# A two-part sequence model on one core: merges of the first block re-ordered and fed early, late convolution taps on GpSimd

## The reference, cut to what matters

```python
y_a = rms_norm(o_gla, norm_w)  * silu(g)      # 4 heads of 64
y_b = rms_norm(o_diff, norm_w) * (1 - lambda_init) * silu(g)   # 4 heads of 128
y_c = rms_norm(o_hgrn, norm_w) * silu(g)      # 4 heads of 64
y = jnp.concatenate([y_a, y_b, y_c], axis=-1) @ w_out[layer]
x = x + rms_norm(y, norm_post[layer])
```

## Time and profile before

| | us |
|---|---|
| median of 3 runs | 4371.12 (4370.69 to 4390.93) |
| the profiled execution | 4380.19 |
| its span, first to last instruction | 4378.4 |
| PE busy | 3314.5 (76%) |
| VectorE (DVE) busy | 2278.0 (52%) |
| ACT busy | 1315.6 (30%) |
| GpSimd (POOL) busy | 492.2 (11%) |

### The profile page before, as it was taken

The page is one execution under the profiler, slowest core; times in us unless marked ns, Lnnn a source line. Parts: engine busy times, 40 slices in busy tenths (PEclk is TensorE's granted clock), DMA queues, the critical chain, the costliest instruction groups (busy, mean ns, idle before and its releaser), DMA issues. The chain is left out here.

```text
span 4378.4 us, 82454 instructions
## 1 busy us (share of the span) xinstructions
PE 3314.5 (76%) x35948; PEld 2727.3 (62%) x35948; DVE 2278.0 (52%) x3684; ACT 1315.6 (30%) x2374; POOL 492.2 (11%) x399
## 2 busy tenths in 40 slices
PE   6998555565769995544749699898776778888499
PEld 6998443244349994442534599797765657777344
DVE  4212984475662216866747512167477845455343
ACT  2111651143331114632433211133244412222341
POOL 0000541110100003421001000000000012222100
PEclk9999656799889995666989899899877869899799
DMA  4232002441332321113123322265422031120331
GB/s 157 87 98 73 21 27 103 152 102 51 114 136 86 99 74 36 31 54 103 39 82 111 132 83 82 104 195 162 160 97 70 33 96 42 42 52 23 146 115 39
DMA packets 260456, 383.97 MB, mean 88 GB/s; under 512 B 46527, under 2 KB 193271, under 8 KB 258684
## 3 DMA queue, kind: packets, MB, share of 16 engines
q1 hardware_dynamic: 155962, 257.35, 18.8%
q10 hardware_dynamic: 104134, 121.36, 8.1%
HBM read 261.66 MB, written 123.13 MB: 88 GB/s over the span
## 5 line engine op out<-in xcount | busy, mean ns | idle before, releaser
L361 PE MATMUL psum<-proj_w_low,h_high 128*128 128x344 f32 (+1 forms) x1984 | 656.5, 331 | 0.0
L361 PE MATMUL psum<-proj_w_high,h_high 128*128 128x344 f32 (+1 forms) x1984 | 654.3, 330 | 0.0
L361 PE MATMUL psum<-proj_w_high,h_low 128*128 128x344 f32 (+1 forms) x1984 | 654.3, 330 | 0.0
L392 DVE COPY proj_y<-psum 128x344 f32<-128x344 f32 (+1 forms) x130 | 70.8, 544 | 782.0 <-PE psum L361 782.0
L361 PEld LDWEIGHTS psum<-proj_w_high,h_high 128*128 128x128 f32 x1984 | 374.8, 189 | 6.6
L361 PEld LDWEIGHTS psum<-proj_w_low,h_high 128*128 128x128 f32 x1984 | 374.6, 189 | 6.0
L361 PEld LDWEIGHTS psum<-proj_w_high,h_low 128*128 128x128 f32 x1984 | 374.3, 189 | 4.5
L417 ACT ACTIVATE proj_y<-psum 128x344 f32<-128x344 f32 (+1 forms) x130 | 61.9, 476 | 694.2 <-PE psum L361 694.2
L800 POOL TENSOR_TENSOR scan_d<-scan_b 128x384 f32<-128x384 f32 x112 | 124.4, 1111 | 1122.4 <-DVE scan_b L646 1115.5
L1312 PE MATMUL psum<-merge_wo,merge_yt 128*128 128x512 f32 x512 | 227.7, 603 | 13.5 <-ACT merge_yt L1257 10.0
L361 PE MATMUL psum<-proj_rest_w_low,h_high 128*128 128x304 f32 x640 | 201.7, 315 | 39.9 <-DVE proj_rest_w_low L381 20.5
(11 more groups left out here) (412 smaller groups left out, 7084.3 us busy)
## 6 DMA issues: line engine op xcount, KB each, us to landing
proj_raw<-in_w_in SPq DMA_DIRECT2D x24, 1376.0 KB, 6.9
proj<-proj_y ACTq DMA_DIRECT2D x192, 172.0 KB, 1.9
delta_x<-dn_qkv SPq DMA_DIRECT2D x40, 384.0 KB, 5.1
proj<-proj_y ACTq DMA_DIRECT2D x68, 224.0 KB, 1.9
dn_prep_x<-proj SPq DMA_DIRECT2D x54, 256.0 KB, 3.6
proj_raw<-in_w_in SPq DMA_DIRECT2D x7, 1792.0 KB, 8.8
norm_x<-x_stream SPq DMA_DIRECT2D x24, 512.0 KB, 3.3
modulate_w<-in_mod_w SPq DMA_DIRECT2D x6, 2048.0 KB, 8.3
```

The lines of the kernel that those rows point to most:

```text
L361: last = PE.matmul(self.ps[:, j % 4, 0:self.width], hp[:, kt, tokens], wp[:, c % 2, kt, :], start=kt == 0 and n == 0, stop=kt == KT - 1 an ...
L392: V.tensor_copy(self.y[:, j % 4, :], self.ps[:, j % 4, 0:self.width]).then_inc(*self.copied[1].inc())
```

## The change

In the first block the weight `w_out` and the constants of a merge get fixed places in SBUF. They are fetched by a stage `Fetch` of six DMAs on SP, woven into the attention ahead of the merge with start 1; `Fetch` waits for them at 10 (so at 11). `Merge1` has no DMA for weight or constants of its own. Its tiles are re-ordered: gates are made two tiles ahead, gates 1 and 2 in one piece after tile 0's copy; the transposes of tile n+1 go ahead of the products of tile n (for tile 1, behind the products of tile 0); `fetch(n + 2)` goes ahead of the load of x.

```diff
-        self.wo, self.hw, self.pw, self.dsc = t("wo", [P, KT, D]), t("hw", [P, D]), t("pw", [P, D]), t("dsc", [P, 1])
+        self.wo, (self.hw, self.pw, self.dsc) = wo, consts
...
-        self.weight, self.consts = sig("dma", "weight", 1), sig("dma", "consts", 14)
...
-        SP, a, L = self.nc.sync, self.a, slice(self.layer, self.layer + 1)
-        for name, w, h0, h1 in (("gla_norm", 64, 0, 4), ("diff_norm", P, 2, 6), ("hgrn_norm", 64, 12, 16)):
-            for h in range(h0, h1):
-                SP.dma_start(self.hw[:, h * w:(h + 1) * w], bc(a[name][L, :], [P, w])).then_inc(*self.consts.inc())
-        SP.dma_start(self.pw[:], bc(a["norm_post"][L, :], [P, D])).then_inc(*self.consts.inc())
-        with self.nc.allow_non_contiguous_dma(reason="one value per partition"):
-            SP.dma_start(self.dsc[:], bc(a["c_layers"][L, 2:3], [P, 1])).then_inc(*self.consts.inc())
+        SP = self.nc.sync
...
         for n in range(NT):
+            if n + 2 < NT:
+                fetch(n + 2)
             if n >= 2:
                 SP.wait_ge(*self.added(n - 2))
             SP.dma_start(self.x[:, n % 2], self.xs[n * P:(n + 1) * P, :]).then_inc(*self.x_loaded[n % 2].inc())
-            if n + 2 < NT:
-                fetch(n + 2)
             yield
...
-        V.wait_ge(*self.consts(13))
         c(V.tensor_scalar(self.hw[:, 256:768], self.hw[:, 256:768], self.dsc[:], None, ALU.mult))
-        for _ in self.dve_gate(0):
-            pass
-        for n in range(NT):
-            V.wait_ge(*self.turned(n))
-            if n >= 2:
-                V.wait_ge(*self.projected(n - 2))
-            V.tensor_copy(self.yt[:, n % 2, 512:1024], self.ps[:, 4 * (n % 2) + 1]).then_inc(*self.copied_v.inc())
-            yield from weave(self.dve_gate(n + 1) if n + 1 < NT else iter(()), self.dve_finish(n - 1) if n else iter(()))
-        yield from self.dve_finish(NT - 1)
-
...
+        self.dve_sums(0)
+        self.dve_gate(0)
+        self.dve_copy(0)
+        for n in (1, 2):
+            self.dve_sums(n)
+            self.dve_gate(n)
+        for n in range(NT + 1):
+            yield n
+            m, s = n - 1, (n - 1) % 2
+            if n + 1 < NT:
+                self.dve_copy(n + 1)
+            if n:
+                V.wait_ge(*self.y_squared(m))
+                V.tensor_scalar(self.ys[:, s:s + 1], self.ys[:, s:s + 1], 1.0 / D, EPS, ALU.mult, ALU.add).then_inc(*self.y_meant.inc())
+            if n and n + 2 < NT:
+                self.dve_sums(n + 2)
+            if n:
+                V.wait_ge(*self.y_rstd(m))
+                V.wait_ge(*self.x_loaded[s](m // 2))
+                V.scalar_tensor_tensor(out=self.y[:, s], in0=self.y_ps(m), scalar=self.ys[:, s:s + 1], in1=self.pw[:], op0=ALU.mult, op1=ALU.mult).then_inc(*self.y_scaled.inc())
+                V.wait_ge(*self.y_scaled(m))
+                V.tensor_tensor(self.y[:, s], self.y[:, s], self.x[:, s], ALU.add).then_inc(*self.added.inc())
+            if n and n + 2 < NT:
+                self.dve_gate(n + 2)
+
+    def dve_copy(self, n):
+        V = self.nc.vector
+        V.wait_ge(*self.turned(n))
+        if n >= 2:
+            V.wait_ge(*self.projected(n - 2))
+        V.tensor_copy(self.yt[:, n % 2, 512:1024], self.ps[:, 4 * (n % 2) + 1]).then_inc(*self.copied_v.inc())
+
...
     def act(self):
         S = self.nc.scalar
-        S.dma_start(self.wo[:], self.a["w_out"][self.layer].rearrange("(k p) n -> p k n", p=P)).then_inc(*self.weight.inc())
-        for _ in self.act_gate(0):
-            pass
-        for n in range(NT):
-            s = n % 2
-            S.wait_ge(*self.turned(n))
-            if n >= 2:
-                S.wait_ge(*self.projected(n - 2))
-            S.activation(self.yt[:, s, 0:512], self.ps[:, 4 * s], ACT.Copy).then_inc(*self.copied_s.inc())
-            yield from weave(self.act_gate(n + 1) if n + 1 < NT else iter(()), self.act_finish(n - 1) if n else iter(()))
...
+        self.act_logs(0)
+        self.act_sigmoid(0)
+        self.act_copy(0)
+        for n in (1, 2):
+            self.act_logs(n)
+            self.act_sigmoid(n)
+        for n in range(NT + 1):
+            yield n
+            m, s = n - 1, (n - 1) % 2
+            ys = self.ys[:, s:s + 1]
+            if n:
+                S.wait_ge(*self.projected(m))
+                if m >= 2:
+                    S.wait_ge(*self.stored[s](m // 2 - 1))
+                S.activation(self.y[:, s], self.y_ps(m), ACT.Square, accum_out=ys).then_inc(*self.y_squared.inc())
+            if n + 1 < NT:
+                self.act_copy(n + 1)
+            if n:
+                S.wait_ge(*self.y_meant(m))
+                self.k.so.chain(S.activation(ys, ys, ACT.Ln))
+                S.activation(ys, ys, ACT.Exp, scale=-0.5).then_inc(*self.y_rstd.inc())
+            if n and n + 2 < NT:
+                self.act_logs(n + 2)
+            if n:
+                S.wait_ge(*self.added(m))
+                S.dma_start(self.xs[m * P:(m + 1) * P, :], self.y[:, s]).then_inc(*self.stored[s].inc())
+            if n and n + 2 < NT:
+                self.act_sigmoid(n + 2)
...
-        PE.wait_ge(*self.weight(0))
-        for n in range(NT):
+
+        def turn(n):
             s = n % 2
...
+        turn(0)
+        for n in range(NT):
+            yield n
+            s = n % 2
+            if n and n + 1 < NT:
+                turn(n + 1)
             PE.wait_ge(*self.copied_s(n))
             PE.wait_ge(*self.copied_v(n))
             if n >= 2:
@@ -1311,9 +1333,8 @@
                 for j in range(8):
                     last = PE.matmul(ps[:, 4 * s + 2 + half], self.yt[:, s, j * P:(j + 1) * P], self.wo[:, j, half * 512:(half + 1) * 512], start=j == 0, stop=j == 7)
             last.then_inc(*self.projected.inc())
-            yield
-
-
+            if n == 0:
+                turn(1)
```

```diff
-        yield 1.6
+        yield self.CONVOLVED
         S.wait_ge(*self.conv(u))
...
+class DeltaPrepareLate(DeltaPrepare):
+
+
+    CONVOLVED = 2.6
+
+    def __init__(self, *args):
+        super().__init__(*args)
+        n = len(self.units)
+        self.tap0, self.tap2, self.tap_added = self.event("pool", "tap0", n), self.event("pool", "tap2", n), self.event("dve", "tap_added", n)
+
+    def pool(self):
+        self.nc.gpsimd.wait_ge(*self.consts(0))
+        yield from self.each(self.pool_unit)
+
+    def pool_unit(self, u):
+        G, s = self.nc.gpsimd, u % 2
+        yield 0
+        G.wait_ge(*self.loaded[s](self.loads[u]))
+        if u >= 2:
+            G.wait_ge(*self.done(u - 2))
+        G.tensor_tensor(self.tmp[:, s], *self.tap(u, 0), ALU.mult).then_inc(*self.tap0.inc())
+        yield 1.3
+        G.wait_ge(*self.tap_added(u))
+        G.tensor_tensor(self.tmp[:, s], *self.tap(u, 2), ALU.mult).then_inc(*self.tap2.inc())
+
+    def convolve(self, u, y, tmp):
+        V = self.nc.vector
+        self.k.vo.chain(V.tensor_tensor(y, *self.tap(u, 1), ALU.mult))
+        yield 1
+        V.wait_ge(*self.tap0(u))
+        V.tensor_tensor(y, y, tmp, ALU.add).then_inc(*self.tap_added.inc())
+        yield 2
+        V.wait_ge(*self.tap_added(u))
+        V.wait_ge(*self.tap2(u))
+        V.tensor_tensor(y, y, tmp, ALU.add).then_inc(*self.conv.inc())
...
-            together(k, (attention, 0, 1.0), *beside)
-            run(k, Merge1(k, layer, p1, o_scan, o_diff, xs))
...
+            fetch = Fetch(k, f"merge1_{layer}", [(wo[:], args["w_out"][layer].rearrange("(k p) n -> p k n", p=P)), *heads,
+                                                 (pw[:], bc(args["norm_post"][one, :], [P, D])), (dsc[:], bc(args["c_layers"][one, 2:3], [P, 1]))])
+            together(k, (attention, 0, 1.0), *beside, (fetch, 1, 1.0))
+            run(k, Merge1(k, layer, p1, o_scan, o_diff, xs, wo, (hw, pw, dsc)))
...
-        together(k, (attention, 0, 1.0), (DeltaPrepare(k, "dn_prep_late", range(6, NT2), p2, dn, attention.top), 2, 1.1))
+        together(k, (attention, 0, 1.0), (DeltaPrepareLate(k, "dn_prep_late", range(6, NT2), p2, dn, attention.top), 2, 1.1))
```

More of the change, by code:

```diff
@@ L1208, in dve_gate, with heads, dve_sums @@
+    def dve_copy(self, n):
[4 more added lines that the diff above has]
+        V.tensor_copy(self.yt[:, n % 2, 512:1024], self.ps[:, 4 * (n % 2) + 1]).then_inc(*self.copied_v.inc())
+    @staticmethod
+    def heads(x, a, b, w):
+        return x[:, a:b].rearrange("p (h d) -> p h d", d=w)
+    def dve_sums(self, n):
+        V, c, s, ss = self.nc.vector, self.k.vo.chain, n % 2, self.ss
         V.wait_ge(*self.o_squared(n))
@@ L1209, in dve_gate @@
         for a, b, w, h in self.HEADS:
-            last = V.reduce_sum(ss[:, s, h:h + (b - a) // w], heads(self.sq, a, b, w), axis=AX)
+            last = V.reduce_sum(ss[:, s, h:h + (b - a) // w], self.heads(self.sq, a, b, w), axis=AX)
         last.then_inc(*self.summed.inc())
@@ L1869, in dve_unit @@
             V.wait_ge(*self.stored[s](self.stores[u - 2]))
[L1870 to L1875 removed]
+        yield from self.convolve(u, y, tmp)
         yield 3.5
```

(12 more changed lines are left out.)

66 lines of the change are left out of this document (23 added, 43 removed).

## The result

The changed kernel took 4312.9 us (median of 4 runs, 4302.5 to 4323.4) against 4374.4 for the kernel before beside it: a ratio of 0.984, 95% interval 0.982 to 0.987. The forecast was 4322. A later comparison on another chip gave 0.986 (0.984 to 0.989). The profiled execution took 4316.56 us, 63.6 less than that of before; the medians lie 61.5 apart. 49.0 were forecast.

The account below looks back on a forecast made before the run. No engine was full overall; late fetches delayed merge starts, TensorE bounded their steady part, and VectorE's convolution work mostly lengthened neighbourhood attention. 47.4 + 0.8 - 1.5 + 2.3 = 49.0 us off 4371.12 gave 4322.1; 8-in-10 range 4302 to 4340.

Parts of the forecast that it names:

- The start of the merges: Both merges: with constants and weight fetched earlier, first gates start 26.1 and 21.3 us sooner, 47.4 us gained.
- The order of the tiles: Merges: 0.83 us a tile gained but used up by two TensorE waits at the start; 0.8 us left in all.
- Beside the attentions: Attentions ahead of the merges: first head delayed 0.5 us, VectorE held longer by the bias addition 1 us; 1.5 us lost.
- The late taps: Neighbourhood attention: two products per unit moved from VectorE to GpSimd gain 12.3 us, less 3, 1 and 6: +2.3 us.
- the prediction's own sign: Listed mark of a wrong forecast: the neighbourhood attention stage at 3163 to 3522 being 10 us shorter or longer.
- the contention: Neighbourhood attention: GpSimd's 24 tap products hold VectorE for an eighth of their 25 us, 3 us lost (0 to 25).
- The wait behind the third pair's addition: Neighbourhood attention: fourth unit's tap 2 queues behind a table addition on GpSimd, holding VectorE 8.8 us; 6 us counted (3 to 9).
- GpSimd's taps pay: Neighbourhood attention: third pair's wait absorbed and taps never meet VectorE, part worth +13 us, time 4311; chance 0.18.
- Taps cost: Neighbourhood attention: taps meet VectorE half the time and the wait costs 9 us, part -10 us, time 4334; chance 0.18.
- VectorE bounds the merge: Merges: VectorE's round is 16 us instead of 14.3, losing 7 to 8 us a merge, time 4337; chance 0.07.
- fetch not hidden: Attentions' first heads delayed 4 us each, addition held badly, merge's first inputs needing 10 us: time 4341; chance 0.05.
- slower than before: Neighbourhood attention: 24 waits for GpSimd hold VectorE over 2.1 us each; at 3 us each, time 4396; chance 0.02.

Follow-up runs that it names:

- e1: Kernel before plus only the early fetch of weight and constants beside the attentions, old tile order and taps: ratio 0.988 to the kernel before.
- e12: Late convolutions' taps 0 and 2 computed by no engine, VectorE making tap 1's product and two additions: 4317.4 us, ratio 0.986 to the kernel before.
- e2: Changed kernel with the late taps back on VectorE, both merge parts kept: ratio 0.987 to the kernel before.
- e4: Changed kernel with GpSimd's tap 2 at 1.1 instead of 1.3, ahead of the third pair's table addition: ratio 0.981 to the kernel before.
- e6: Changed kernel with tap 2 at 1.1 and GpSimd's bias addition cut into 8 pieces: ratio 0.981 to the kernel before.
- e10: Repeat of the changed kernel with tap 2 at 1.1 and the bias addition in 8 pieces: 4295.8 us, ratio 0.981 to the kernel before.
- e3: Kernel before with only the late taps moved to GpSimd: ratio 0.995 to the kernel before.
- e9: The changed kernel run again, unaltered: 4312.3 us, ratio 0.986 to the kernel before.
- e11: Repeat of the changed kernel with the late taps back on VectorE: 4323.0 us, ratio 0.988 to the kernel before.
- e7: Changed kernel with tap 2 at 1.1, later pairs' five transfers 1.5 steps apart and table additions behind them: ratio 0.983 to the kernel before.

## Why the forecast was right, point by point

**The start of the merges** was the right place and the right size: 6.6 us to the first gate were forecast, 7.0 and 6.2 came; transposes at 18.4, 18.7 and 17.9 came. e1 shows that the fetch is 49 of the 50 us that the two merges lost.

**The order of the tiles.** With T = 1098.24, the start of the first transposes, gate 2 ends at T + 23.4 as worked out, TensorE waits 3.92 us (4.0), tile 2's products start at T + 40.9 (41.2), the round is 14.61 (14.8) and the last products end at T + 127.0 (127.9). The second wait, 1.8 us, is hidden in the first merge by tile 1's products, which took 14.9 instead of 13.8 us (the granted clock was 0.63 in their first 2.7 us, and 1.00 from 1126 on); in the second merge there are 2.53 and 2.85 us of waiting and the end is T + 128.0. So 0.4 us a merge was small by a microsecond (1.4 measured), and the reason given for so little holds: most of the steady gain of a microsecond a tile is spent on waits at the start. There VectorE's gates 2 and 3 are the limit. In the steady part VectorE as the bound of the merge is excluded: gates 4 to 6 end 0.8 us ahead of their transposes in both merges, where half a microsecond was forecast.

**Beside the attentions.** -1.5 was forecast, and 1.7 us were lost in the first pair. In the mean of all profiles the first attention is 2.5 us longer with the fetch than without (249.9 us in eight against 247.4 in three; the addition in one piece in all of them). The 0.5 us for a delayed head came from no row, and no run shows it: in the second attention, which has it without the addition, nothing is seen (234.2, 237.2 and 235.8 us in the three kernels without it, 234.1 to 237.4 in those with it). What it does is to move the addition to another place in VectorE's step, and how long it holds VectorE is then chance: 11.4, 11.8 and 11.9 us without the fetch, and 11.3, 11.3, 11.4, 12.0, 14.5, 14.6, 15.6 and 16.3 with it (mean 13.4; 12.4 was my guess). The stage roughly follows: 247 to 248 us at 11.3, 254 at 16.3. That the first pair came so close to the guess is luck.

**The late taps** are where the sum was off, by 9.0 us (2.3 forecast, 11.3 in the mean of the profiles). By the prediction's own sign, a stage 10 us shorter or longer, this part was wrong. Four terms were mis-sized. The first is the quarter of VectorE's products that I took to be hidden: 12.3 should have been 16.4, and e12 measures 16.6; my own count of steps (84 us of extra work, 94 of extra time) said so. The second is the contention, 3 us: L1904, the instruction that mostly met a tap, was stretched in two or three of the 12 units, by 1.3 to 2.8 us in all in the eight kernels, but the stage is not longer by it. What the Trainium skill states in "SBUF — State Buffer", section "Who interferes with whom", agrees with the single instruction: in e2 VectorE's product is held for the 16.33 us of the addition. The loss of about 20 us that I had worked out for every tap meeting one of VectorE's instructions was far from this stage: they seldom meet. The third is the microsecond for ACT, of which nothing is seen. The fourth is the wait. The wait behind the third pair's addition was forecast in its place and mechanism; it lasts 11.24 us instead of 8.8, as a tap takes 1.27 us and VectorE comes to it 7.6 us ahead of the addition's start where I had 5.4, and it costs 7.9 (e4, e6, e10 against e3, e9 and the changed kernel) where I had 6. A tap of 1.27 us should have been seen too: I had taken 1.04 from the earlier trace rows, another stage's product. The sum of the terms as measured is 16.6 - 7.9 = 8.7, against 11.3 from the means. No run explains the 2.6 us between them; stages that vary by 5 to 7 us within a group allow no more.

**The rest of the 63.6 us.** 8.8 us came from stages in which nothing was edited, 6.2 of them from the delta stage. They were in no term of the forecast. The delta stage's instructions are the same in all kernels, and VectorE, ACT and GpSimd are busy for the same time; TensorE is not, and the granted clock differs with it (0.89, 0.87 and 0.92 below). Delta stages of before, e1 and the changed kernel:

```profile
3522.39:4078.94 556.55, 466.77 (x15564) 406.19 (x15564) 263.82 (x545) 112.23 (x242) 116.61 (x100) 0.89 0.20 51
```

```profile
3478.22:4050.88 572.66, 479.50 (x15564) 416.95 (x15564) 264.62 (x545) 112.17 (x242) 116.51 (x100) 0.87 0.20 49
```

```profile
3465.59:4015.98 550.39, 454.39 (x15564) 394.22 (x15564) 264.19 (x545) 112.17 (x242) 116.53 (x100) 0.92 0.20 51
```

So of the 14.6 us by which the pair of profiles goes beyond the forecast, 4.2 are the neighbourhood stage, 8.8 are these and 1.8 are the merges, while the attentions take 0.2 back. What stays open is whether the taps have a part in it. With taps on GpSimd the delta stage took 543.8 to 557.2 us (8 profiles, mean 550.7), without 554.7 to 572.7 (6 profiles, mean 560.8). e11 was to test it and at 554.7 lies between what either reading said; e12, also without them, took 558.3. Ten microseconds in a stage that begins behind a barrier, by a clock that no edit touches: I know of no mechanism, and the runs show none. It would explain why e3's ratio, 0.995, is 20 us and not 11. Against it stands that e9 and e11 differ in time by 10.8 us, which the neighbourhood stage alone accounts for. It stays open.

**The rivals.** "GpSimd's taps pay" (4311) came nearest to the median of 4312.9. That is in part luck: its price of 13 us is near the 11.3 measured, but 8.8 us of the gain in the profile come from unedited stages that no rival had in it, and its reason is only half right. The taps hardly met VectorE's instructions, as it said, but the stall was there. "Taps cost", "VectorE bounds the merge", "fetch not hidden" and "slower than before" fell; of 24 waits for GpSimd one held VectorE.

## What to carry to other kernels

Constants and weights that a stage needs first are worth fetching in the stage before, and what this gives can be read off the trace to a microsecond: first input landed against first constant landed. When an in-order engine takes on a second job, look through its queue for the one place where the new instruction stands behind one that waits for something else; here one number of one instruction was worth 8 us. When a wait goes, look at what would have ended next: here a store stood 3.6 us behind the table. And if an engine's extra time is as long as its extra work, count the work in full.

## What the runs showed of the hardware

A long GpSimd addition over SBUF (16.4 us) held a VectorE product of single columns until it ended (0.22 us became 11.3 to 16.3, in 11 profiles), while reductions and copies out of PSUM went on at 1.22 and 0.69 us. In pieces of 2.4 us the same work held VectorE for 6 us instead of 11 to 16. A product of the same shape, 128x512, takes 1.04 us on GpSimd in the delta stage and 1.27 for a tap. And beside the fourth pair's transfers a store takes 7.9 to 8.1 us to land instead of 2.0, whether they are issued in one burst (e4) or in portions (e7); issuing them in portions left 10.7 of 11.6 us of waiting.
